# Spreading modulation rows over partitions with TensorE from SBUF instead of with row loads from DRAM

## The reference

```
shift1, scale1, gate1, shift2, scale2, gate2 = split(silu(cond) @ w_mod + b_mod, 6)   # one row of 1024 each, for c_ctx and for c
h = x * (1 + scale1) + shift1
q, k, v, ... = split(h @ w_in)          # three kinds of attention or retention heads
y = concat(heads) @ w_out
x = layer_norm(ALPHA * x + gate1 * y, ln1_w, ln1_b)
h = x * (1 + scale2) + shift2
y = moe(h)                              # 32 experts, two per token, SwiGLU, 1024 -> 256 -> 1024
x = layer_norm(ALPHA * x + gate2 * y, ln2_w, ln2_b)
```

## Time and profile before

| | us |
|---|---|
| median of 3 runs | 1126.06 |
| lowest, highest | 1124.64, 1127.91 |
| the profiled execution, its own time | 1121.87 |
| its span, first to last instruction | 1120.0 |
| TensorE busy | 1049.8 (94%) |
| VectorE busy | 430.1 (38%) |
| ScalarE busy | 215.9 (19%) |
| moved by the DMA engines | 342.79 MB, mean 306 GB/s |

### The profile page before, as it was taken

How to read it: one execution, slowest core, us unless ns; L and a number is a source line. 1 busy time by engine, 2 the same in 40 slices (tenths; PEclk the granted TensorE clock), 3 DMA queues, 4 the chain that set the end, 5 groups by cost and what they waited for, 6 DMA issues and landing times.

```text
span 1120.0 us, 16760 instructions
## 1 busy us (share of the span) xinstructions
PE 1049.8 (94%) x6678; PEld 697.5 (62%) x6679; DVE 430.1 (38%) x1075; ACT 215.9 (19%) x536; POOL 178.2 (16%) x183
## 2 busy tenths in 40 slices
PE   5999999999999999979999999999999999999875
PEld 0865877658856565545548567785687656555532
DVE  0034645346764221121154445452668522212115
ACT  0322324301011111101112323341001111111111
POOL 0133302023101111111111200200511111111101
PEclk8999999999999999999999999999999999999998
DMA  8966942489799999999989922225897999999993
GB/s 354 271 147 129 382 173 90 144 284 349 300 420 419 418 418 419 419 417 419 419 310 264 310 75 76 90 76 195 297 413 300 377 419 419 418 419 418 418 398 159
DMA packets 102626, 342.79 MB, mean 306 GB/s; under 512 B 20300, under 2 KB 61308, under 8 KB 70420
## 3 DMA queue, kind: packets, MB, share of 16 engines
q1 hardware_dynamic: 88400, 313.47, 72.6%
q0 software_dynamic: 12416, 18.79, 5.6%
q10 hardware_dynamic: 1732, 9.45, 2.1%
HBM read 337.76 MB, written 28.25 MB: 327 GB/s over the span
## 4 chain that ended last, share of the span: by engine, by line
PE 70%; DMA 14%; SPq 6%; DVE 5%; ACT 2%; issue 2%; POOL 1%; ACTq 0%; POOLq 0%; DVEq 0%
PE ps L1058 17%; PE ps L1365 11%; PE ps L1051 9%; SPq L910 6%; PE ps L1389 5%; DMA expert_rows<-arena 4%; PE ps L998 3%; PE ps L1242 3%; DMA ring<-in_exp_w_down 3%; DMA arena<-in_exp_w_down 3%; DMA arena<-in_exp_w_up 3%; PE ps L1234 2%; DMA ring<-in_w_mod 2%; PE ps L1332 2%; PE ps L1440 2%
## 5 line engine op out<-in xcount | busy, mean ns | idle before, releaser
L1058 PE MATMUL ps<-ring,arena 128*128 128x256 f32 (+1 forms) x960 | 197.2, 363 | 2.1 <-ACT arena L1689 2.1
L1365 PE MATMUL ps<-ring,arena 128*64 128x256 f32 x1264 | 183.6, 381 | 11.7 <-ACT arena L1751 7.0
L1058 PEld LDWEIGHTS ps<-ring,arena 128*128 128x128 f32 x960 | 168.4, 192 | 24.4 <-issue 5.1
L1365 PEld LDWEIGHTS ps<-ring,arena 128*64 128x64 f32 x1264 | 113.6, 137 | 59.7 <-ACT arena L1751 9.2
L1051 PE MATMUL ps<-arena,ring 128*128 128x384 f32 x288 | 96.9, 490 | 0.5 <-ACT arena L1694 0.5
L1365 PE MATMUL ps<-arena 128*64 128x256 f32 x512 | 93.7, 381 | 1.2 <-ACT arena L1751 0.9
L1389 PE MATMUL ps<-ring,arena 128*64 128x512 f32 x296 | 89.6, 614 | 5.1 <-DMA ring<-in_exp_w_down 4.2
L2278 DVE TENSOR_TENSOR arena<-arena,ps 128x256 f32<-128x256 f32 x32 | 13.5, 421 | 190.8 <-ACT arena L1756 190.8
L2563 POOL DMA_INDIRECT arena<-token_rows,arena x30 | 30.7, 1022 | 310.8 <-PE ps L1332 140.9
L1051 PEld LDWEIGHTS ps<-arena,ring 128*128 128x128 f32 x288 | 53.3, 190 | 36.6 <-issue 1.8
L2285 DVE COPY arena<-ps 128x512 f32<-128x512 f32 x32 | 22.1, 691 | 124.7 <-PE ps L1389 73.5
(11 more groups left out here) (311 smaller groups left out, 1462.8 us busy)
## 6 DMA issues: line engine op xcount, KB each, us to landing
ring<-in_exp_w_gate SPq DMA_DIRECT2D x45, 1024.0 KB, 23.8
ring<-in_w_mod SPq DMA_DIRECT2D x43, 1024.0 KB, 6.9
ring<-in_exp_w_down SPq DMA_DIRECT2D x38, 1024.0 KB, 25.9
ring<-in_exp_w_up SPq DMA_DIRECT2D x36, 1024.0 KB, 25.8
ring<-in_w_in SPq DMA_DIRECT2D x24, 1024.0 KB, 12.9
arena<-in_exp_w_up SPq DMA_DIRECT2D x17, 1024.0 KB, 23.9
arena<-in_exp_w_gate SPq DMA_DIRECT2D x15, 1024.0 KB, 28.0
arena<-in_exp_w_down SPq DMA_DIRECT2D x15, 1024.0 KB, 28.2
```

The lines of the kernel that those rows point to most:

```text
L1058: mm = pe.matmul(out[:, 0:w], hT[:, ch, where * P:(where + 1) * P], unit(l, name)[:, ch, 0:w], start=(ch == 0), stop=(ch == CH - 1))
L1365: mm = pe.matmul(ps[64 * w:64 * w + 64, i % 2, kind * FF:(kind + 1) * FF], xgT[:, ch, w * SLOTS:(w + 1) * SLOTS], weights[:, ch * FF:(ch + ...
```

## The change

TensorE spreads the rows. The stationary operand is a column of the identity, repeated 128 times, over a few partitions; it picks one of these partitions and gives its 512 (or 256) values to all 128 output partitions.

In the front there are three rounds (`spread_rows`): round 0 behind "out" 0 and ahead of "scores" 2 gives gate1 and shift2 of the context, round 1 behind "out" 2 and ahead of the last two slices gives them for the latents, round 2 behind the first half of `out_local` gives scale2 of both. Each is four products, from the four partition groups of `modrow_l` into four banks, and four copies on ScalarE (`copy_spread`) into the same places as before. TensorE waits for copies of round 0 before "scores" 2, of round 1 before the first `out_local`, of round 2 before tile 1's. SP still loads ln1's two rows.

For the late rows the sources (gate2's two rows from `modrow_l`, by four small DMAs that ScalarE issues; ln2's two rows from the input, by two small DMAs of SP) are collected in the last 256 columns of the `bias` tile, 16 KB: four partitions for each row, 256 values on each. In the last pair of experts TensorE makes two rounds of eight products (`late_rows`), one ahead of the gate products and one between them and the up products, with four copies each on ScalarE ahead of its silu. `row_act` and `row_dve` become one semaphore.

```diff
-ROWS_LATE = {1: ("gate1", "shift2"), 2: ("scale2", "gate2")}
...
-    for n, step in ((4, ("states", 0)), (2, ("scores", 0)), (2, ("scores", 1)), (0, ("out", 0)), (3, ("scores", 2)),
-                    (0, ("out", 1)), (3, ("out", 2)), (len(late), None)):
+    for n, step in ((4, ("states", 0)), (2, ("scores", 0)), (2, ("scores", 1)), (0, ("out", 0)), (0, ("spread", 0)), (3, ("scores", 2)),
+                    (0, ("out", 1)), (3, ("out", 2)), (0, ("spread", 1)), (len(late), None)):
...
+SPREAD_BANKS = ((2, 3, 7, 5), (0, 2, 3, 7), (2, 3, 4, 5))
+LATE_BANKS = ((PAIRS - 2) % 2, 2, 3, MARKS_BANK)
...
-                store_rows(l, 1)
-                load_rows(l, "gate1")
-                load_rows(l, "ln1")
-                store_rows(l, 2)
-                load_rows(l, "ctx2")
-                load_rows(l, "lat2")
+                load_rows(l)
+                load_late(l)
...
+            def load_late(l):
+
+                wait_released(sp, l, ("arena", BIAS_PLACE))
+                for k, row in enumerate((ln2_w, ln2_b)):
+                    sp.dma_start(late_source()[32 * (2 + k):32 * (2 + k) + 4, :],
+                                 row[l, :].rearrange("(q n) -> q n", q=4)).then_inc(bias_in.sem, 16)
...
                 if t == 2:
                     pe.wait_ge(sc_ready.sem, sc_ready.at(l, 1))
+                    pe.wait_ge(spread_copied.sem, spread_copied.at(l, 1))
...
+            def spread_rows(l, r):
+
+                b = 1 if r < 2 else 2
+                wait_drained(pe, l, JOB_NO["mod", b, CH - 1])
+                if r:
+                    pe.wait_ge(spread_copied.sem, spread_copied.at(l, r))
+                for n, bank in enumerate(SPREAD_BANKS[r]):
+                    g, k = (n, r) if r < 2 else (n % 2, n // 2)
+                    col = K_ID + 32 * g + k
+                    mm = pe.matmul(ps[:, bank, :], kc[32 * g:32 * g + 2, col:col + 1].to_broadcast([2, P]),
+                                   modrow_l[b - 1][32 * g:32 * g + 2, :], start=True, stop=True)
+                mm.then_inc(spread_ready.sem, 1)
...
+                if t == 1:
+                    pe.wait_ge(spread_copied.sem, spread_copied.at(l, 3))
...
                 if t == 0 and units[0] == 0:
                     pe.wait_ge(ret_done.sem, ret_done.at(l, TILES))
+                    pe.wait_ge(spread_copied.sem, spread_copied.at(l, 2))
...
+            def late_rows(l, n):
+
+                if n == 0:
+                    pe.wait_ge(bias_in.sem, bias_in.at(l, bias_in.step))
+                    pe.wait_ge(pt_copied.sem, pt_copied.at(l, 1))
+                    pe.wait_ge(hid_ready.sem, hid_ready.at(l, PAIRS - 1))
+                    pe.wait_ge(xt_act.sem, xt_act.at(l, PAIRS))
+                    pe.wait_ge(xt_dve.sem, xt_dve.at(l, PAIRS))
+                else:
+                    pe.wait_ge(late_copied.sem, late_copied.at(l, 1))
+                for q in range(2):
+                    for g in range(4):
+                        rows4 = slice(32 * g, 32 * g + 4)
+                        col = K_ID + 32 * g + 2 * n + q
+                        mm = pe.matmul(ps[:, LATE_BANKS[g], 256 * q:256 * q + 256], kc[rows4, col:col + 1].to_broadcast([4, P]),
+                                       late_source()[rows4, :], start=True, stop=True)
+                mm.then_inc(late_ready.sem, 1)
...
+                    if i == PAIRS - 1:
+                        late_rows(l, 0)
                     hidden(l, i, 0)
+                    if i == PAIRS - 1:
+                        late_rows(l, 1)
...
                 out_local(l, 0, (0, 1))
+                spread_rows(l, 2)
                 mix_T(l, 0)
...
+            def copy_spread(l, r):
+
+                act.wait_ge(spread_ready.sem, spread_ready.at(l, r + 1))
+                for n, bank in enumerate(SPREAD_BANKS[r]):
+                    k = r if r < 2 else n // 2
+                    if r < 2:
+                        name, row = (("gate1", k), (("ctx2", "lat2")[k], 1))[n // 2]
+                    else:
+                        name, row = ("ctx2", "lat2")[k], 0
+                    if n % 2 == 0:
+                        wait_released(act, *SPOT[l, ("rows", name)][2])
+                    ins = act.activation(row_tile(l, name, row)[:, 512 * (n % 2):512 * (n % 2) + 512], ps[:, bank, :], ACT.Copy)
+                ins.then_inc(spread_copied.sem, 1)
...
+                act.wait_ge(job_act.sem, job_act.at(l, job_act.step))
+                for k in range(2):
+                    for h in range(2):
+                        part = 64 + 32 * h + k
+                        act.dma_start(late_source()[32 * k + 2 * h:32 * k + 2 * h + 2, :],
+                                      modrow_l[1][part:part + 1, :].rearrange("p (q n) -> p q n", q=2)).then_inc(bias_in.sem, 16)
+                copy_spread(l, 2)
...
                     if i == PAIRS - 2:
                         rows_half(l, i)
+                        copy_late_rows(l, 0)
+                        copy_late_rows(l, 1)
...
                 dve.wait_ge(rows_in.sem, rows_in.at(l, rows_in.step))
+                dve.wait_ge(spread_copied.sem, spread_copied.at(l, 3))
...
-                dve.wait_ge(gate2_in.sem, gate2_in.at(l, gate2_in.step))
+                dve.wait_ge(late_copied.sem, late_copied.at(l, 2))
```

More of the change, by code:

```diff
@@ L546, in row_tile, with late_source @@
             return places_of_unit[SPOT[l, ("rows", name)][0]][:, k * D:(k + 1) * D]
+        def late_source():
+            return bias[:, :, :, :].rearrange("p h r c -> p (h r c)")[:, UNIT:UNIT + 256]
         def late_tile(l, name, k):
@@ L690, in build @@
         down_ready = signal("down_ready", PAIRS, start=1)
-        row_act, row_dve = signal("row_act", PAIRS, start=1), signal("row_dve", PAIRS, start=1)
+        row_copied = signal("row_copied", 2 * PAIRS, start=1)
         o_full = [signal(f"o_full{s}", 16) for s in range(ITEM_UNITS)]
@@ L809, in _ @@
             sp.dma_start(condraw[:, 1, :], c.rearrange("o (p c) -> p (o c)", p=P)).then_inc(cond_in.sem, 16)
[L811 to L846, removed]
+            def load_rows(l):
+                wait_released(sp, *SPOT[l, ("rows", "ln1")][2])
+                for k, row in enumerate((ln1_w, ln1_b)):
+                    sp.dma_start(row_tile(l, "ln1", k), row[l:l + 1].to_broadcast([P, D])).then_inc(rows_in.sem, 16)
@@ L883, in bias_loads @@
                     wait_released(sp, *LAST_IN[l - 1][BIAS_PLACE])
+                    sp.wait_ge(late_copied.sem, late_copied.at(l - 1, 2))
                 one = bass.ds(l, 1)
@@ L967, in _ @@
                                 load_item(l, o0, i)
-                    elif unit[0] == "late":
-                        load_late(l, unit[1])
-                    elif unit[0] != "item" and unit[0] != "gath":
+                    elif unit[0] not in ("item", "gath", "late"):
                         load(l, unit)
@@ L1568, in _ @@
                         ret_out(l, i)
+                    elif kind == "spread":
+                        spread_rows(l, i)
                 out_local(l, 0, (0, 1))
+                spread_rows(l, 2)
                 mix_T(l, 0)
@@ L1773, in rows_half, with copy_late_rows @@
                     act.wait_ge(rows_out[(i - 1) % 2].sem, rows_out[(i - 1) % 2].at(l, 16 * ((i + 1) // 2)))
-                act.activation(result_rows(i)[:, 0:512], ps[:, 5, :], ACT.Copy).then_inc(row_act.sem, 1)
+                act.activation(result_rows(i)[:, 0:512], ps[:, 5, :], ACT.Copy).then_inc(row_copied.sem, 1)
+            def copy_late_rows(l, n):
+                act.wait_ge(late_ready.sem, late_ready.at(l, n + 1))
+                if n == 0:
+                    for name in ("gate2", "ln2"):
+                        wait_released(act, *SPOT[l, ("late", name)][2])
+                for g in range(4):
+                    ins = act.activation(late_tile(l, ("gate2", "ln2")[g // 2], g % 2)[:, 512 * n:512 * n + 512],
+                                         ps[:, LATE_BANKS[g], :], ACT.Copy)
+                ins.then_inc(late_copied.sem, 1)
             def marks_of_last(l):
@@ L1823, in _ @@
                         swish(l)
-                one = bass.ds(l, 1)
+                    elif kind == "spread":
+                        copy_spread(l, i)
+                act.wait_ge(job_act.sem, job_act.at(l, job_act.step))
[5 more added lines that the diff above has]
+                copy_spread(l, 2)
                 for t in range(TILES):
@@ L1832, in _ @@
                 act.wait_ge(results_out.sem, results_out.at(l, results_out.step))
+                act.wait_ge(bias_in.sem, bias_in.at(l, bias_in.step))
                 for t in range(TILES):
```

34 lines of the change are left out of this document (12 added, 22 removed).

## The result

The changed kernel takes 1132.97 us, median of 10 runs (1127.63 to 1135.22), against 1124.11 us of the kernel before beside it (10 runs, 1122.28 to 1127.91). The ratio is 1.0075, 95% interval 1.0061 to 1.0089, so the kernel is slower: +8.9 us as the difference of the two medians, +8.4 us by the ratio (6.9 to 10.0). One single execution of all that are reported here, of the kernel with shortened row loads, ran in a slow state (1784.79 us at a clock of 0.557) and is left out. The changed kernel moves 332.27 MB instead of 342.79 MB. It became slower although its DMA engines have 10.5 MB less to do.

The account below looks back on a forecast made before the run. TensorE's front, setting each layer's weight-stream restart, was taken as the bound. Terms of 2.4 + 1.6 us in layer 0 and 2.4 + 0 in layer 1 gave +6.4, on 1126.06 making 1132.5 us (+0.57%); range 1124 to 1143.

Parts of the forecast that it names:

- Bytes are free ahead of the dry spot: End of each layer's front, DMA share 0.19 and 0.04: taking 3.15 MB out ahead of it saves 0.
- Rival 1: Each layer: bytes are time, the front's 3.15 MB comes off the end, 7.5 us each, 1111 us; chance 0.14.
- A spread of four row groups, 1.06 us: In the front: four products from four partition groups overlap, 0.86 us plus 0.2 on top.
- Three spreads of s, "3s - 0.75 = +2.4": Each layer's front: three rounds of 1.06 us, less 0.75, delay TensorE by 2.4 us, with no idle time behind.
- rival 2: Front and late rows: row groups run only in pairs (1141 us) or one after another (1156); chance 0.15.
- The copies of the second spread, +0.25 net: Before `out_local`: ScalarE's copies take 2.17 us, two slices cover 1.92; `out_local` starts 1.4 us later.
- Late rows, +1.6 in layer 0: Last expert pair: of 2.1 us for two rounds some 0.5 hidden in layer 0, +1.6; layer 1, 0.
- Rival 3: Front copies hidden; layer 0's late rows have 2.6 us of room without the clock fall at 503: 1129.3; chance 0.11.
- VectorE: In layer 0's front: rows ready 3.9 us earlier, tile 0 can start 1 us earlier, wait for logits longer.
- The four small DMAs on ScalarE: Ahead of the third round's copies: 0.33 us each, issued before that spread is ready; uncovered they would cost 1.3.
- The signs: In the profile after: `out_local` waiting for a ScalarE copy, first `out_rest` and the DMA engines' idle stretch's end 2.4 us later.
- The sign of being wrong: In the front: the weight stream restarting at the old time, or a spread taking 2 us or more.

Follow-up runs that it names:

- kernel with shortened row loads: Kernel before, six row loads per layer cut from 1024 to 8 values per partition, rows wrong; 1116.23 us, median of five, against 1124.29.
- second measurement: The changed kernel, unaltered, measured once more beside later runs; 1131.49 us against 1124.52 of the kernel before, ratio 1.0071.
- late rows alone: Kernel before with only gate2 and ln2 spread by TensorE, front rows still loaded from DRAM; 1124.57 us against 1123.52, ratio 1.0011.
- plain products: Kernel before with full 128-row products in the places of the three spreads, no copies or waits; 1130.90 us against 1124.29, ratio 1.0057.
- 32 rows: Changed kernel with front products of 32 rows in place of 2; 1130.76 us against 1123.52 of the kernel before, ratio 1.0059.
- front alone: Changed kernel with gate2 and ln2 loaded from DRAM as before, only the front's three spreads new; 1134.19 us, ratio 1.0085 to the kernel before.
- second spread behind: Changed kernel with the second spread behind the last two modulation slices instead of ahead; 1138.07 us against 1123.52 of the kernel before, ratio 1.0128.
- four-group variant: The kernel with 32 rows, third spread reading gate2's quarters from four row groups, results wrong; one execution, fronts 26.33 and 26.32 us.
- 8 rows: Changed kernel with front products of 8 rows in place of 2; one execution, 1130.09 us, fronts 27.17 and 27.17.

## Why the prediction came out as it did

The time, 1132.97 against 1132.5, and the sign are right, and so is the mechanism: the front of TensorE sets the restart of the stream. Its price was not: a front grew by 4.80 us and not by 2.4. That the number agrees to 0.5 us is luck. The prediction was +6.4 us from a median of 1126.06; the kernel before measured 1124.11 beside the changed one, and the difference was +8.9 (+7.0 in the second measurement). A base 1.9 us too high met a sum 2.5 us too low. Within the sum one term was too small (the third spread), one was missing (the clock), and one was too large (the late rows).

The mechanism first. Twice the growth of the front, beside the measured difference of the medians (all timed with the kernel before beside them; the intervals are 1.4 to 2.4 us either way, and every growth lies inside the interval of its kernel):

| kernel | front, layers 0 and 1 | growth, both | measured |
|---|---|---|---|
| late rows alone | 23.61, 23.62 | 0.0 | +1.1 |
| plain products | 26.90, 26.89 | 6.6 | +6.6 |
| 32 rows | 27.18, 27.17 | 7.1 | +7.2 |
| changed kernel | 28.41, 28.39 | 9.6 | +8.9 |
| front alone | 28.40, 28.41 | 9.6 | +10.7 |
| second spread behind | 31.92, 30.46 | 15.2 | +14.6 |

So TensorE's time ahead of the last `out_rest` goes into the kernel's time one for one, as closely as these times can tell. The second measurement of the changed kernel, with one fall instead of two in its profile, has 27.17 and 28.40, 8.4 together, beside +7.0.

*Bytes are free ahead of the dry spot*: right (fronts unchanged with 3.1 MB less per layer, and with 3.1 MB more), and what bytes cost behind it was seen as well: 6.8 us in the trace for 3.15 MB, where the price of the prediction gives 7.5. Rival 1 was excluded.

*A spread of four row groups, 1.06 us*: right for the first two (1.07) and for the late ones (1.08). The Trainium skill (TensorE: Matmul & The Clock Gate, section "Measured speedup vs the span model") gives 3.07 times for four row groups at 512 columns; an estimate from that is 1.12 us. The trace agrees nearly, with 3.2 times: 1.07 us, against the 3.44 that were estimated for one after another.

*Three spreads of s, "3s - 0.75 = +2.4"*: this term was mis-sized, and the mistake lay in reading the code. The third spread reads scale2, which lies in groups 0 and 1 alone (`n % 2`); its four products share two groups and cost 1.92 us, the pairs' price that rival 2 named for all of them (1.72 + 0.2). The four-group variant gives the 0.85 back. Rival 2 was thus true of one spread in three.

*The copies of the second spread, +0.25 net*: right in size. Where the clock doesn't fall, `out_local` waits 0.38 us, and its start shifts by 1.5 (the prediction: 1.4). With the cover gone the wait is 2.23 us (the prediction: 2.17). The Trainium skill (TensorEngine Tiling (Array Packing), section "PSUM Bottleneck") warns that behind a fourfold speedup the copy out of PSUM may become the bottleneck. The trace agrees where nothing covers the copies, with 2.23 us of waiting behind 1.14 us of products. They are hidden where three slices cover them: the second pair of copies of the first spread ended 0.6 us ahead of the scores that wait for them (predicted: 0.7).

*Not foreseen: the clock.* Behind the second spread it falls to 0.51, and two slices take 3.52 us to the start of `out_local` instead of 1.85, +1.67, of which 0.4 would otherwise have been the wait for copies. Net 1.23 us per front where it falls. The prediction had looked for falls only where TensorE waits. The sum for a front: 1.07 + 1.07 + 1.92 of spreads, less 0.99 of idle time that they cover, plus 1.67 is 4.74; measured 4.80.

*Late rows, +1.6 in layer 0*: too large. In the two kernels looked at above it is 0 by the trace (the last pair starts at the same distance from the front), and +1.1 (-0.3 to +2.7) by the times. I took the wait of 0.24 us ahead of the last pair as all the room that TensorE had. That wait was short because in that execution the clock had been at 0.60 from 503 us and TensorE had come late. Rival 3 named this, and it goes both ways. The eight kernels with late spreads have 16 layer ends. In eight of them TensorE still waits 0.83 to 1.07 us for weights behind the second late spread, and no fall of the clock stands in the 60 us ahead of it; among these are both layers of the changed kernel in its first profile. In the other eight the clock fell within these 60 us (0.60 from 506 to 510 in the changed kernel's second profile, for one), TensorE came late, and there is no such wait. There the last down product starts 301.41 to 302.36 us behind the first `out_rest` in layer 0, where the kernel before has 301.37, and 277.24 to 277.73 in layer 1, where it has 276.71. So the late rows cost nothing or up to 1.0 us a layer, in layer 1 too, where the prediction had them hidden.

*VectorE*: half right. The rows came 1.46 us earlier (268.12 less 1.36, against 268.22) and not 3.9, since the front was longer than predicted, and nothing was gained by it. But the wait for the logits did not grow, 3.11 as before; the freed time appeared earlier, as 2.24 us ahead of tile 0. *The four small DMAs on ScalarE* took 0.75 us each (2.99 for four) and not 0.33; they ended at 264.89, 0.9 us before the third spread was done, so it didn't show.

*The signs*: the dry spot ended 4.80 us later and not 2.4, and `out_local` waited for no copy in the first profile, because the slow slices covered them. The sign of being wrong, a spread of 2 us or more, was missed narrowly by the third, 1.92.

Left open: what it is about 2-row products that the clock reacts to, and why it spared one front of eight. The falls at other places (near 317 and 503 us in the kernel before, near 493 in the changed one) move from kernel to kernel, and what each is worth in the end was not separated. No variant here beats the kernel before. The late rows alone can't be told from it. Of the kernels that spread the front's rows and leave them right, the one with 32 rows is 7.2 us slower and the one with 8 rows 5.6 in its one execution, and the 4.06 us of the three spreads, less the 0.99 that they cover, would stay in each front even if nothing waited for a copy.

## What to carry to other kernels

Before taking bytes off the DMA engines, find the stretch in which they stand still: bytes ahead of it were free here, and so was the round trip through DRAM, because the work that ended the stretch didn't wait for either. Moving that trip onto the engine that ends the stretch is then a pure loss, whatever the profile says of waits elsewhere. When products are to run side by side in row groups, count for each call the groups in which its operands really lie, and try small selector products with more rows than they need, the added selector entries zero, where the rows are there (8 cost the same time as 2). And an experiment that makes data wrong may change data-dependent work: count the DMAs before believing its time.

## What the runs showed of the hardware

- Four float32 products of 512 columns from four row groups into four banks took 1.07 us, with 2, 8 or 32 rows alike; the same four from two groups 1.92 us.
- The granted clock fell to half directly behind such a spread with 2 rows in 7 of 8 fronts (0.51 in the profile above), without any idle time of TensorE before it, and in none of 6 with 8 or 32 rows, nor behind full 128-row products (2 fronts).
- A spread of 2 rows earlier in the same front, at 242.09, was followed by no fall, and neither was the third one at 263.91.
- Small DMAs from SBUF to SBUF issued by ScalarE took 0.75 us each of its queue (2.99 for four), where row loads on SP took 0.42 to 0.44 (0.83 for two, 1.75 for four).
- An expert's three weight units, 3.15 MB, taken out of the full stream ended layer 0's stream 6.8 us earlier.
